# Where the normed values lie, and latents before context in the joint projections

## The chip, the cores and the metric

The kernel runs on one core of a Trainium2 chip. The metric is the time of one execution in device microseconds (us); three runs of the kernel before took 2563.52 to 2567.49 us, median 2566.14. Lower is better. TensorE multiplies matrices (a product streams up to 512 columns of a "moving" operand past 128x128 loaded values); VectorE, ScalarE and GpSimd work elementwise; SyncE issues the transfers.

## The reference

Two blocks in a row on 512 latent tokens beside 256 context tokens, model width 1024, float32. The first block has a feed-forward network, a mixer of retention and gated linear attention, and a second network (latents alone); the second has a matrix-memory mixer of four heads and one attention layer. Each stage begins with a norm, scaled and shifted by a condition, and its result is what all projections of the stage read:

```python
def rms_norm(x, w):
    y = xf * lax.rsqrt(jnp.mean(xf * xf, axis=-1, keepdims=True) + EPS)
    return (y * w.astype(jnp.float32)).astype(x.dtype)
def modulate(h, shift, scale):
    return h * (1.0 + scale[:, None, :]) + shift[:, None, :]
def swiglu(h, w1, w3, w2):
    return (jax.nn.silu(h @ w1) * (h @ w3)) @ w2
...
x = x + 0.5 * m_l[2] * swiglu(modulate(rms_norm(x, norm1_w[i]), m_l[0], m_l[1]), ffn1_w1[i], ffn1_w3[i], ffn1_w2[i])
ctx = ctx + 0.5 * m_c[2] * swiglu(modulate(rms_norm(ctx, norm1_w[i]), m_c[0], m_c[1]), ...)
y_l, y_c = token_mixing(modulate(rms_norm(x, norm2_w[i]), ...), modulate(rms_norm(ctx, norm2_w[i]), ...), w_in[i], ...)
```

## The kernel before, in words

Values lie by feature: 8 tiles k of 128 features, and 768 columns, of which 0 to 255 are context (CTX) and 256 to 767 latents (LAT). Every large product is made of three, for accuracy: an operand is split into a high part that TensorE takes as fp32r, and a low part (the rest). The normed values are hh and hl, weights wh and wl, and the product is wh·hh + wh·hl + wl·hh. In a network's second projection u (uh, ul) takes the place of h; in the matrix-memory block m_yh and m_yl, in retention r_yh and r_yl.

Weights come in chunks of 256 columns (m). SyncE loads chunk m into one of two stage buffers, ScalarE writes wh (L385), VectorE wl (L393), and each waits until the buffer's chunk before, m-2, is used. `by_features` (L411) multiplies a chunk: for each half f (128 of its columns), for each k, for each of the three terms, first the context's 256 columns into half of bank b[2] (L444), then the latents' 512 columns into bank b[f] (L447). Two sets of three banks, SETS, take turns. After a half, the semaphore gemm for (m, f) is raised, and after both also that of m; whoever reads the context waits for that of m. Between the halves `mid` is called, and after each k `beside`, which let small products of other work in. With `ready` (the first chunk on new values) the latents of both halves come first (L422), then the context (L434), each k waiting for its values.

Where only latents are wanted, L447 stands alone: in the second network, for retention's queries, keys and gates, and in attention (L3617). Products with tokens as loaded operand (L1556, L4089) move the weights. The joint form, context and latents in turn, has 2112 pairs on hh and hl: 20 chunks of the first network, one of the gated attention's keys (GK), 7 chunks of keys and queries and 16 of output gates in the matrix-memory block, 48 pairs a chunk. It has 324 pairs on u and 288 on m_y.

In the matrix-memory block `ml_pe` (L3298) multiplies for each head h the keys' chunk (MK), the gate rows (L2903, `gate_rows_pe`), and the queries' chunk (MQ). For h of 1 to 3 MQ has as `mid` `normed_output_pe` (L3128): two products of ones and a diagonal matrix, which spread the scale of the previous head's output. They wait for m_out_diag, which VectorE raises at L3126, after the reciprocal L3124, after ScalarE's root (L553). ScalarE comes to that root, in program order, after the wh of a chunk that waits for MK's end, the copies of keys, the gate rows and the exponentials of the gate's weights.

In memory each partition's buffers follow one another from byte 1152. By that arithmetic stage, wh, wl, direct, hh and hl begin on multiples of 128 bytes, and rows and token tiles in them too. The shared area, in which u, r_y and m_yh lie (and at times two weight buffers, third), begins 32 bytes behind such a multiple. The attention's output a_yh lies where hh does.

Of the kernel before, what the change touches and what calls it, by code (L numbers as in the profile page):

```python
# [3 lines left out]
T = 768  # L4
C = 256
L = 512
# [221 lines left out]
        self.n, self.counted = 0, True  # L228


class Tally:


# [7 lines left out]
def build(nc, wts, vec, con, conds, xin, cin, cin2, out):  # L241
# [5 lines left out]
    F32, F32R = mybir.dt.float32, mybir.dt.float32r  # L247
# [13 lines left out]
    base = 1152  # L261

    def at(name, shape, dt, off):
        return nc.alloc_sbuf_tensor_at(name, shape, dt, offset=base + off)

    x = at("x", [128, 8, T], F32, 0)
    o = 24576
# [3 lines left out]
    o += 16384  # L271
    wl = [at(f"wl{i}", [128, 2048], F32R, o + 8192 * i) for i in range(2)]
    o += 16384
    DIRECT = o
    direct = [at(f"direct{i}", [128, 1024], F32, o + 4096 * i) for i in range(3)]
    o += 12288
    HREG = o
    hh = at("hh", [128, 8, T], F32R, o)
    hl = at("hl", [128, 8, T], F32R, o + 24576)
    o += 49152  # L280
    con0 = at("con0", [128, 512], F32, o)
    o += 2048
    vecs = at("vecs", [128, NVEC], F32, o)
# [12 lines left out]
    MVA = o  # L296
    o += 4096
    cb = at("cb", [128, 8, 6], F32, o)
    o += 192
    AREA = o  # L300
    ASIZE = 228192 - o

    def area(name, shape, dt, off):
        n = 4
# [10 lines left out]
    bank = [stack.enter_context(nc.psum_tensor(f"ps{i}", [128, 512], F32)) for i in range(8)]  # L315
    CTX, LAT = slice(0, C), slice(C, T)
# [33 lines left out]
    group = [area(f"group{i}", [128, 8, 256 * len(g)], F32, 16384 * i) for i, g in enumerate(GROUPS)]  # L350
    group_in = [[signal(f"group_in{i}_{j}", 16) for j in range(4 if i == 0 else 2)] for i in range(len(GROUPS))]

    rows_at = [DIRECT, DIRECT + 4096, DIRECT + 8192, AREA + 40960, AREA + 45056, HREG + 18432]
    rows_chunk = [at(f"first{i}", [128, 1024], F32, o_) for i, o_ in enumerate(rows_at)]
    rows_chunk_in = [signal(f"first_in{i}", 16) for i in range(len(rows_at))]

# [5 lines left out]
    gemm = signal("gemm")  # L362
# [41 lines left out]
    def empty(pe, *banks):  # L404
        for b in banks:
            if emptied[b]:
                s, key = emptied[b]
                pe.wait_ge(*s.at(*key))
                emptied[b] = None

    def by_features(pe, m, b, sh, sl, lat, ctx, ready=None, mid=None, beside=None):  # L411

        nk, h, l = parts(m)
        pe.wait_ge(*w_low.at(m))
        empty(pe, *([b[0], b[1]] if lat else []), *([b[2]] if ctx else []))
        if ready:

            for k in range(nk):
                ready(0, k)
                for f in range(2):  # L420
                    for a, (w, s) in enumerate(((h, sh), (l, sh), (h, sl))):
                        i = pe.matmul(bank[b[f]][:, :], w[:, k, 128 * f:128 * f + 128], s[:, k, LAT], start=k == 0 and a == 0,  # L422
                                      stop=k == nk - 1 and a == 2, skip_group_check=True)
            i.then_inc(*gemm.up(m, 0))
            gemm.also(m, 1)
            gemm.also(m)
            if mid:
                mid()
            if ctx:
                for f in range(2):  # L430
                    for k in range(nk):
                        ready(1, k)
                        for a, (w, s) in enumerate(((h, sh), (l, sh), (h, sl))):
                            i = pe.matmul(bank[b[2]][:, 256 * f:256 * f + 256], w[:, k, 128 * f:128 * f + 128], s[:, k, CTX],  # L434
                                          start=k == 0 and a == 0, stop=k == nk - 1 and a == 2, skip_group_check=True)
                i.then_inc(*gemm.up(m))
            return
        for f in range(2):
            cols = slice(128 * f, 128 * f + 128)
            for k in range(nk):  # L440
                for a, (w, s) in enumerate(((h, sh), (h, sl), (l, sh))):
                    st, en = k == 0 and a == 0, k == nk - 1 and a == 2
                    if ctx:
                        i = pe.matmul(bank[b[2]][:, 256 * f:256 * f + 256], w[:, k, cols], s[:, k, CTX], start=st, stop=en,  # L444
                                      skip_group_check=True)
                    if lat:
                        i = pe.matmul(bank[b[f]][:, :], w[:, k, cols], s[:, k, LAT], start=st, stop=en, skip_group_check=True)  # L447
                if beside and k < nk - 1:
                    beside((nk - 1) * f + k)
            i.then_inc(*gemm.up(m, f))  # L450
            if f == 0 and mid:
                mid()
        gemm.also(m)

    def by_tokens(pe, m, b, sh, sl, tiles, mid=None):

# [39 lines left out]
    class Norm:  # L496


        def __init__(self, n, lo, off, slot, parts=None):
            self.n, self.lo, self.slot, self.parts = n, lo, slot, parts  # L500
            self.acc = area(f"n_acc{n}", [128, T], F32, off)
            self.sq = [area(f"n_sq{i}_{n}", [128, T], F32, off + 3072 * (i + 1)) for i in range(2)]
            self.dg = area(f"n_dg{n}", [128, T], F32, off + 9216)
            NORMS[n] = self
# [152 lines left out]
    sq1 = [area(f"n_sq1_{i}", [128, T], F32, 55296 + 3072 * i) for i in range(4)]  # L657
    factor1 = area("factor1", [128, T], F32, 67584)

    row1 = [at(f"row1_{i}", [128, 512], F32, HREG + 43008 + 2048 * i) for i in range(2)]  # L660
    M1first = M1[:, 0:16, :].rearrange("p (a k) s -> p a k s", a=2)
    bias_first = bias1[:, 0:32].rearrange("p (a k s) -> p a k s", a=2, k=8)
    row_copied = signal("row_copied")
# [789 lines left out]
    o = (o + 64 + 31) // 32 * 32  # L1453
# [481 lines left out]
    class Lat:  # L1935
# [5 lines left out]
        def __getitem__(self, i):  # L1941
            p, k, s = i
            return self.t[p, k, s.start - C:s.stop - C]
# [1549 lines left out]
    o = 25088  # L3493
# [857 lines left out]
```

## Time and profile before

| | |
|---|---|
| three runs, median | 2566.14 us |
| the profiled execution, and its span | 2565.66 us, 2563.9 us |
| TensorE busy | 2523.1 us, 98% |
| VectorE, ScalarE, GpSimd busy | 1301.4, 824.4, 229.3 us |
| chain that ended last | TensorE 92%, VectorE 5%, ScalarE 2% |
| mean granted clock of TensorE | 0.996 |

The span is the profiled stretch, 1.8 us less than the execution's own time. A product's length in the trace reaches over the next one's start, since products are pipelined: the pace is read from the starts. Starts of single rows are given to 0.01 us, so a pace is read best from two rows far apart with a known number of products between them. A row of the timeline with a count joins several instructions of one kind.

### The profile page before, as it was taken

What the parts mean: (1) busy time and instruction counts of PE and PEld (TensorE: products, weight loads), DVE (VectorE), ACT (ScalarE), POOL (GpSimd) and SP (SyncE); (2) the same over time, 40 slices, a digit from 0 to 9 for tenths busy, and PEclk for the clock granted to TensorE, in tenths of its full rate; (3) what the DMA queues carried; (4) which work ended last, traced back from release to release, by engine and by line L of the source; (5) the groups of instructions that cost most, each with busy time, mean ns of one, the idle gap of its engine ahead of it and who ended that gap; (6) DMA issues with size and microseconds to landing.
All of it is one profiled execution on the core that took longest, in us unless ns stands there. A gap on an engine that the chain in (4) does not pass through costs nothing.

```text
span 2563.9 us, 31059 instructions
## 1 busy us (share of the span) xinstructions
PE 2523.1 (98%) x13030; PEld 2019.1 (79%) x13030; DVE 1301.4 (51%) x2065; ACT 824.4 (32%) x1172; POOL 229.3 (9%) x186
## 2 busy tenths in 40 slices
PE   7999999999999999999999999999999999999999
PEld 3888888888757878888888687887787788687766
DVE  6665433426346766767747433422432332476663
ACT  3211112124243354232324323122222312245663
POOL 0100001002111002000000110110210101210001
PEclk9999999999999999999999999999999999999999
DMA  7334343312111112545432110210111021011001
GB/s 294 115 134 157 128 152 119 128 50 82 59 42 65 52 50 81 183 174 191 162 115 91 50 42 17 74 66 17 50 66 50 17 83 66 17 67 66 34 34 50
DMA packets 45114, 223.55 MB, mean 87 GB/s; under 512 B 4736, under 2 KB 6960, under 8 KB 30128
## 3 DMA queue, kind: packets, MB, share of 16 engines
q1 hardware_dynamic: 43008, 215.24, 23.5%
q10 hardware_dynamic: 1968, 6.34, 0.7%
q8 instruction: 103, 1.69, 0.3%
q14 instruction: 35, 0.29, 0.0%
HBM read 219.46 MB, written 2.10 MB: 86 GB/s over the span
## 4 chain that ended last, share of the span: by engine, by line
PE 92%; DVE 5%; ACT 2%; issue 1%; POOL 0%; DMA 0%; SPq 0%; DVEq 0%; ACTq 0%; POOLq 0%
PE ps L447 41%; PE ps L444 13%; PE ps L1556 8%; PE ps L422 3%; PE ps L3617 3%; PE ps L3164 3%; PE ps L2953 2%; PE ps L1257 2%; PE ps L876 1%; PE ps L3734 1%; PE ps L3833 1%; PE ps L3857 1%; DVE wl L393 1%; PE ps L2543 1%; PE ps L2079 1%
## 5 line engine op out<-in xcount | busy, mean ns | idle before, releaser
L393 DVE TENSOR_TENSOR wl<-stage,wh 128x2048 fp32r<-128x2048 f32 (+2 forms) x155 | 325.8, 2102 | 478.7 <-ACT wh L385 478.5
L447 PE MATMUL ps<-hh,wh 128*128 128x512 f32 x1120 | 442.0, 395 | 0.0
L447 PE MATMUL ps<-hl,wh 128*128 128x512 f32 x1120 | 441.4, 394 | 0.0
L447 PE MATMUL ps<-hh,wl 128*128 128x512 f32 x1120 | 441.1, 394 | 0.0
L385 ACT ACTIVATE wh<-stage 128x2048 fp32r<-128x2048 f32 (+2 forms) x155 | 267.2, 1724 | 456.3 <-PE ps L447 338.5
L447 PEld LDWEIGHTS ps<-hh,wl 128*128 128x128 f32 x1120 | 210.5, 188 | 48.5
L447 PEld LDWEIGHTS ps<-hh,wh 128*128 128x128 f32 x1120 | 210.6, 188 | 47.2 <-issue 1.2
L447 PEld LDWEIGHTS ps<-hl,wh 128*128 128x128 f32 x1120 | 210.4, 188 | 47.4 <-issue 1.2
L650 DVE CUSTOM_DVE_ANT_0 left<-direct,cond_rows,vecs 128x1024 bf16<-128x1024 f32 x168 | 207.0, 1280 | 0.0
L444 PE MATMUL ps<-hh,wh 128*128 128x256 f32 x688 | 197.6, 287 | 1.2 <-DVE m_X L2977 1.2
L444 PE MATMUL ps<-hh,wl 128*128 128x256 f32 x688 | 194.1, 282 | 0.0
L444 PE MATMUL ps<-hl,wh 128*128 128x256 f32 x688 | 192.9, 280 | 0.0
L444 PEld LDWEIGHTS ps<-hh,wh 128*128 128x128 f32 x688 | 130.6, 190 | 5.7 <-issue 5.5
L444 PEld LDWEIGHTS ps<-hh,wl 128*128 128x128 f32 x688 | 130.0, 189 | 0.0
L444 PEld LDWEIGHTS ps<-hl,wh 128*128 128x128 f32 x688 | 130.0, 189 | 0.0
L1556 PE MATMUL ps<-wh,hh 128*128 128x512 f32 x288 | 119.1, 413 | 0.0
L1209 POOL TENSOR_TENSOR ul<-sl,uh 128x768 fp32r<-128x768 f32 (+1 forms) x28 | 43.6, 1575 | 819.9 <-ACT uh L1097 819.8
L1556 PE MATMUL ps<-wh,hl 128*128 128x512 f32 x288 | 113.4, 394 | 0.0
L1556 PE MATMUL ps<-wl,hh 128*128 128x512 f32 x288 | 113.3, 394 | 0.0
L447 PE MATMUL ps<-uh,wh 128*128 128x512 f32 x240 | 94.6, 394 | 0.0
L1097 ACT ACTIVATE uh<-sl 128x512 fp32r<-128x512 f32 (+1 forms) x42 | 30.7, 734 | 198.2 <-DVE sl L1160 138.2
L447 PE MATMUL ps<-ul,wh 128*128 128x512 f32 x240 | 94.3, 393 | 0.0
(608 smaller groups left out, 4723.7 us busy)
## 6 DMA issues: line engine op xcount, KB each, us to landing
stage<-wts SPq DMA_DIRECT2D x110, 1024.0 KB, 4.8
direct<-wts SPq DMA_DIRECT2D x104, 512.0 KB, 4.2
stage<-wts SPq DMA_DIRECT2D x24, 768.0 KB, 4.3
stage<-wts SPq DMA_DIRECT2D x22, 512.0 KB, 3.3
group<-wts SPq DMA_DIRECT2D x6, 512.0 KB, 6.3
first<-wts SPq DMA_DIRECT2D x6, 512.0 KB, 9.7
x<-xin SPq DMA_DIRECT2D x4, 512.0 KB, 7.7
group<-wts SPq DMA_DIRECT2D x2, 1024.0 KB, 9.7
```

The source lines that it names most:

```text
L385: act.activation(split(m)[0][:, 0:w], stage[m % 2][:, 0:w], ACT.Copy).then_inc(*w_high.up(m))
L393: dve.tensor_tensor(l[:, 0:w], stage[m % 2][:, 0:w], h[:, 0:w].bitcast(F32), SUB).then_inc(*w_low.up(m))
L422: i = pe.matmul(bank[b[f]][:, :], w[:, k, 128 * f:128 * f + 128], s[:, k, LAT], start=k == 0 and a == 0, stop=k == nk - 1 and a == 2, skip ...
L444: i = pe.matmul(bank[b[2]][:, 256 * f:256 * f + 256], w[:, k, cols], s[:, k, CTX], start=st, stop=en, skip_group_check=True)
L447: i = pe.matmul(bank[b[f]][:, :], w[:, k, cols], s[:, k, LAT], start=st, stop=en, skip_group_check=True)
L650: dve.tensor_tensor_reduce(left[n % 2][:, :], chunk[:, :], rows_of[:, s, :], 1.0, bias[:, s:s + 1], MUL, ADD, to[:, s:s + 1]).then_inc(*mo ...
L1209: pool.tensor_tensor(z.ul[:, k, z.lo:T], z.sl[(2 * p + f) % 4][:, z.lo:T], z.uh[:, k, z.lo:T].bitcast(F32), SUB).then_inc(*u_low_pool.up(n ...
L1257: j = pe.matmul(bank[tail_bank(i, ft)][:, 0:p.n], w[:, k, cols], s[:, k, p.cols], start=k == 0 and a == ends[0], stop=k == 3 and a == ends ...
L1556: i = pe.matmul(bank[t][:, :], s[:, 4 * j + k, 128 * t:128 * t + 128], u[:, k, :], start=j == 0 and k == 0 and a == 0, stop=j == 1 and k = ...
L2953: i = pe.matmul(bank[bb][:, 0:hi_ - lo], mk[:, f, 128 * J:128 * J + 128], mq[:, f, lo:hi_], start=f == 0, stop=f == 1, skip_group_check=True)
L3164: pe.matmul(bank[b[0]][:, :], mv_[:, J, fs], wpart(J, C, T), start=J == 0, stop=J == 5, skip_group_check=True)
L3617: i = pe.matmul(bank[f][:, :], u[:, k, 128 * f:128 * f + 128], s[:, k, LAT], start=k == 0 and a == 0, stop=k == 7 and a == 2, skip_group_c ...
```

## The change

1. `hh` and `hl` become pairs of tiles, wrapped in a class `Sides` that picks by column: latents hhl and hll, [128, 8, 512], on multiples of 128 bytes, and context hhc and hlc, [128, 8, 256], 64 bytes behind one. 
2. `direct` moves by 64 bytes. The shared area is put on a multiple of 64; worked out as above it begins 64 bytes behind a multiple of 128, where it was 32 behind. The buffers of the first rows (rows_at, row1) move so that they still lie over tiles of h that are written late.
3. In the joint form of `by_features` the latents of both halves come first, then the context of both. `mid` and `beside` stay beside the latents. The semaphore of m is raised after the context, as its readers need.

```diff
+class Sides:
+
+    def __init__(self, tiles):
+        self.context, self.latents = tiles
+
+    def __getitem__(self, i):
+        p, k, s = i
+        if s.stop <= C:
+            return self.context[p, k, s]
+        return self.latents[p, k, slice(s.start - C, s.stop - C)]
+
+
...
-    DIRECT = o
-    direct = [at(f"direct{i}", [128, 1024], F32, o + 4096 * i) for i in range(3)]
-    o += 12288
+    DIRECT = o + 64
+    direct = [at(f"direct{i}", [128, 1024], F32, DIRECT + 4096 * i) for i in range(3)]
+    o += 12416
     HREG = o
-    hh = at("hh", [128, 8, T], F32R, o)
-    hl = at("hl", [128, 8, T], F32R, o + 24576)
-    o += 49152
+    hh = Sides([at("hhc", [128, 8, C], F32R, o + 32832), at("hhl", [128, 8, L], F32R, o)])
+    hl = Sides([at("hlc", [128, 8, C], F32R, o + 41024), at("hll", [128, 8, L], F32R, o + 16384)])
+    o += 49280
...
     cb = at("cb", [128, 8, 6], F32, o)
-    o += 192
+    o += 192 + (-(base + o + 192)) % 64
     AREA = o
-    ASIZE = 228192 - o
+    ASIZE = 228224 - o
...
-    rows_at = [DIRECT, DIRECT + 4096, DIRECT + 8192, AREA + 40960, AREA + 45056, HREG + 18432]
+    rows_at = [DIRECT, DIRECT + 4096, DIRECT + 8192, AREA + 40960, AREA + 45056, HREG + 12288]
...
-        empty(pe, *([b[0], b[1]] if lat else []), *([b[2]] if ctx else []))
+        empty(pe, b[0], b[1], *([b[2]] if ctx else []))
...
             cols = slice(128 * f, 128 * f + 128)
             for k in range(nk):
                 for a, (w, s) in enumerate(((h, sh), (h, sl), (l, sh))):
-                    st, en = k == 0 and a == 0, k == nk - 1 and a == 2
-                    if ctx:
-                        i = pe.matmul(bank[b[2]][:, 256 * f:256 * f + 256], w[:, k, cols], s[:, k, CTX], start=st, stop=en,
-                                      skip_group_check=True)
-                    if lat:
-                        i = pe.matmul(bank[b[f]][:, :], w[:, k, cols], s[:, k, LAT], start=st, stop=en, skip_group_check=True)
+                    i = pe.matmul(bank[b[f]][:, :], w[:, k, cols], s[:, k, LAT], start=k == 0 and a == 0, stop=k == nk - 1 and a == 2,
+                                  skip_group_check=True)
                 if beside and k < nk - 1:
                     beside((nk - 1) * f + k)
             i.then_inc(*gemm.up(m, f))
             if f == 0 and mid:
                 mid()
         gemm.also(m)
+        if ctx:
+            for f in range(2):
+                cols = slice(128 * f, 128 * f + 128)
+                for k in range(nk):
+                    for a, (w, s) in enumerate(((h, sh), (h, sl), (l, sh))):
+                        i = pe.matmul(bank[b[2]][:, 256 * f:256 * f + 256], w[:, k, cols], s[:, k, CTX], start=k == 0 and a == 0,
+                                      stop=k == nk - 1 and a == 2, skip_group_check=True)
+            i.then_inc(*gemm.up(m))
...
-    row1 = [at(f"row1_{i}", [128, 512], F32, HREG + 43008 + 2048 * i) for i in range(2)]
+    row1 = [at(f"row1_{i}", [128, 512], F32, HREG + 28672 + 2048 * i) for i in range(2)]
```

Engines other than TensorE have the same instructions in the same order. On TensorE the number of products is the same too. In the order of TensorE's instructions, at the second pair of chunks of the first network, one k of the joint form reads before (hh_59 and hl_60 are the moving operand, wh0_52 and wl0_54 the loaded one, ps2 the bank of the context, ps0 that of a half's latents; the digits behind are the program's numbering):

```order
L444 MATMUL ps2<-hh_59,wh0_52 128x256
L447 MATMUL ps0<-hh_59,wh0_52 128x512
L444 MATMUL ps2<-hl_60,wh0_52 128x256
L447 MATMUL ps0<-hl_60,wh0_52 128x512
L444 MATMUL ps2<-hh_59,wl0_54 128x256
L447 MATMUL ps0<-hh_59,wl0_54 128x512
```

and now, where the same chunk's latents end and its context begins (ps1 is the bank of the second half's latents):

```order
L454 MATMUL ps1<-hhl_60,wh0_52 128x512
L454 MATMUL ps1<-hll_62,wh0_52 128x512
L454 MATMUL ps1<-hhl_60,wl0_54 128x512
L467 MATMUL ps2<-hhc_59,wh0_52 128x256
L467 MATMUL ps2<-hlc_61,wh0_52 128x256
L467 MATMUL ps2<-hhc_59,wl0_54 128x256
```

The 24 context products of each half have moved from between the latents to behind both halves.

In head 1 of the matrix-memory block, around the call between the halves of the queries' chunk (m_EM holds the diagonal, con the ones), it reads before:

```order
L447 MATMUL ps3<-hl_60,wh1_53 128x512
L444 MATMUL ps5<-hh_59,wl1_55 128x256
L447 MATMUL ps3<-hh_59,wl1_55 128x512
L3131 MATMUL ps6<-m_EM_192,con0_61 128x512
L3132 MATMUL ps7<-m_EM_192,con0_61 128x256
L444 MATMUL ps5<-hh_59,wh1_53 128x256
L447 MATMUL ps4<-hh_59,wh1_53 128x512
```

and now:

```order
L454 MATMUL ps3<-hhl_60,wh1_53 128x512
L454 MATMUL ps3<-hll_62,wh1_53 128x512
L454 MATMUL ps3<-hhl_60,wl1_55 128x512
L3147 MATMUL ps6<-m_EM_194,con0_63 128x512
L3148 MATMUL ps7<-m_EM_194,con0_63 128x256
L454 MATMUL ps4<-hhl_60,wh1_53 128x512
L454 MATMUL ps4<-hll_62,wh1_53 128x512
```

Ahead of that call stood 48 products of the chunk, and now stand 24, the latents alone.

## Rows read from the trace of the kernel before

**Rows 1.** The page: TensorE busy; the chain that ended last, by engine, line
```profile
PE 2523.1 (98%) x13030; PEld 2019.1 (79%) x13030; DVE 1301.4 (51%) x2065; ACT 824.4 (32%) x1172; POOL 229.3 (9%) x186
...
PE 92%; DVE 5%; ACT 2%; issue 1%; POOL 0%; DMA 0%; SPq 0%; DVEq 0%; ACTq 0%; POOLq 0%
PE ps L447 41%; PE ps L444 13%; PE ps L1556 8%; PE ps L422 3%; PE ps L3617 3%; PE ps L3164 3%; PE ps L2953 2%; PE ps L1257 2%; PE ps L876 1%; PE ps L3734 1%; PE ps L3833 1%; PE ps L3857 1%; DVE wl L393 1%; PE ps L2543 1%; PE ps L2079 1%
```

**Rows 2.** By line and form, TensorE: count, busy us, mean ns, idle
```profile
L447 PE MATMUL ps<-hh,wh 128*128 128x512 f32 x1120 | 442.0, 395 | 0.0
...
L447 PE MATMUL ps<-uh,wh 128*128 128x512 f32 x240 | 94.6, 394 | 0.0
```

**Rows 3.** TensorE's timeline, first FFN, pairs in turn: start us, length us
```profile
199.12 0.28 PE L444 MATMUL ps<-hh,wh 128*128 128x256 f32 x1
...
300.88 0.40 PE L422 MATMUL ps<-uh,wh 128*128 128x512 f32 x1
```

**Rows 4.** TensorE's timeline, an output gate of the matrix-memory block, in turn
```profile
1686.48 0.28 PE L444 MATMUL ps<-hl,wh 128*128 128x256 f32 x1
...
1693.77 0.28 PE L444 MATMUL ps<-hl,wh 128*128 128x256 f32 x1
```

**Rows 5.** TensorE's timeline, second FFN, latents alone: of u, then of h
```profile
1062.13 0.40 PE L422 MATMUL ps<-uh,wh 128*128 128x512 f32 x1
...
1095.73 0.40 PE L447 MATMUL ps<-hh,wh 128*128 128x512 f32 x1
...
1150.17 0.39 PE L2628 MATMUL ps<-con,c_acc 128*128 128x1 f32 x3
```

**Rows 6.** TensorE's timeline, first FFN: context of u alone, then pairs
```profile
309.29 0.28 PE L434 MATMUL ps<-uh,wh 128*128 128x256 f32 x1
...
313.53 0.28 PE L444 MATMUL ps<-uh,wh 128*128 128x256 f32 x1
...
350.97 0.28 PE L444 MATMUL ps<-hh,wh 128*128 128x256 f32 x1
```

**Rows 7.** TensorE's timeline, attention values: 256 columns of weights moving
```profile
2275.81 0.28 PE L4089 MATMUL ps<-wh,hh 128*128 128x256 f32 x1
...
2278.69 0.59 PE L3563 MATMUL ps<-a_ksq,con 128*128 128x512 f32 x1
```

**Rows 8.** TensorE's timeline, head 1: gate rows, first half of queries, spread
```profile
1582.43 1.55 PE L2903 MATMUL ps<-m_RR,c_sel 8*128 8x512 f32 x4
1583.91 0.39 PE L444 MATMUL ps<-hh,wh 128*128 128x256 f32 x1
...
1592.35 0.61 PE L3131 MATMUL ps<-m_EM,con 128*128 128x512 f32 x1
```

**Rows 9.** Timelines of ScalarE and of VectorE in the same time
```profile
1582.54 1.06 ACT L385 ACTIVATE wh<-stage 128x1024 fp32r<-128x1024 f32 x1 [11.17 <-PE ps L447]
...
1589.43 1.28 ACT L553 ACT_TABLE_LOAD   x1
1590.73 0.21 ACT L553 ACTIVATE cb<-cb 128x6 f32<-128x6 f32 x1
...
1590.97 0.19 DVE L3124 RECIPROCAL cb<-cb 128x6 f32<-128x6 f32 x1 [3.45 <-ACT cb L553]
1591.19 0.96 DVE L558 TENSOR_TENSOR m_EM<-con,cb 128x768 f32<-128x768 f32 x1
```

**Rows 10.** TensorE's timeline near the start: a pause, products after it
```profile
27.53 0.41 PE L835 MATMUL ps<-con,row 2*128 2x2 f32 x4 [0.68 <-ACT row L711]
30.81 0.47 PE L876 MATMUL ps<-hh,wh 128*128 128x512 f32 x1 [2.88 <-DVE hl L789]
...
35.48 0.63 PE L876 MATMUL ps<-hl,wh 128*128 128x512 f32 x1
35.91 0.63 PE L876 MATMUL ps<-hh,wh 128*128 128x512 f32 x1
```

**Rows 11.** Window of that stretch: busy us by engine, granted clock (0.50), DMA
```profile
31.90:38.60 6.70, 5.09 (x16) 3.79 (x15) 5.82 (x7) 4.39 (x5) 0.00 (x0) 0.50 1.02 409
```

## The prediction

> **What bounds the kernel now.** I read the page's busy times first, then the chain of waits. TensorE is busy for 98% of the span and carries 92% of the chain, over half of it at the two lines of the joint form and of latents alone, L447 and L444 [rows 1]. So the time is the number of products times their pace, and a change that keeps the number can only act through the pace, or through a pause. The lengths in the groups by line (395 and 394 ns [rows 2]) are no pace, since products overlap. I read the paces off the timeline, from the starts of rows far apart and the count between them, all at the full clock of 2.4 GHz (the span's mean granted clock is 0.996):
>
> - context and latents in turn, hh and hl: 288 pairs in 101.76 us, 353.3 ns a pair [rows 3]; in other chunks 21 pairs in 7.29 us, 347.1 ns [rows 4];
> - latents of u alone, 32 bytes behind a multiple of 128: 144 in 33.60 us, 233.3 ns; of hh and hl alone, on the multiple: 240 in 54.44 us, 226.8 ns [rows 5];
> - 256 columns alone: 36 of u in 4.24 us, 117.8 ns [rows 6]; 24 on a multiple of 128, 2.88 us, 120.0 ns [rows 7];
> - u in turn: 108 pairs in 37.44 us, 346.7 ns [rows 6].
>
> At 2.4 GHz 512 and 256 columns are 213.3 and 106.7 ns. The rest, 13 to 20 ns for latents, is what depends on place and order. These are the two things that the change touches.
>
> **Part 1, latents first.** The 2112 pairs of the joint form on hh and hl become 2112 latent products alone, at their old place, whose pace the trace has (226.8 ns), and 2112 context products alone, 64 bytes behind a multiple, whose pace no row has. Call it c. Bounds: below, 106.7 ns, the columns at the full clock. Above, the aligned 120.0, and if 64 is worse than any place seen, as much more as u's latents pay for theirs (6.5 ns), 126.5. The nearest rows are the 117.8 at 32 bytes and the 120.0 at none; the one farther from the multiple is faster, and I take 116.5, a little on from it. Reading each chunk of the timeline, 1296 pairs run at the pace of [rows 3] and 816 at that of [rows 4] (output gates of heads 1 to 3, the second chunk of those heads, GK, and the chunk whose weights lie in the area). So 1296 x (353.3 - 226.8 - 116.5) = 1296 x 10.0 = 13.0 us, and 816 x 3.8 = 3.1 us. The 324 pairs of u gain 346.7 - 343.3 = 3.4 ns if their latents come to 226.8 (next part), 1.1 us; the 288 of m_y are taken like them, 1.0 us.
>
> **Part 2, the area 64 behind instead of 32.** 924 latent products read the area alone (L422 240, L447 396 of u and 96 of r_y, the two tails 192). They run at 233.3 ns where aligned ones run at 226.8 [rows 5]. Bounds at 64: no gain (233.3) or the aligned pace, with one step more the other way, 239.8, as the far end. 2048 bytes from an offset of 32 touch one 64-byte stretch more than from 0, and from 64 they don't; one such stretch is 16 columns, 6.7 ns, which is just the difference. I take 226.8: 924 x 6.5 = 6.0 us. The 492 products of 256 columns there (108 + 96 + 192 + 96) go from 117.8 to 116.5, 0.6 us.
>
> The Trainium skill speaks against both parts. "SBUF — State Buffer", Door 1, gives SBUF 16-byte cachelines: 32 and 64 are both multiples of 16, so by that rule the offset is worth nothing, the sum loses its 6.0 and 0.6, and context keeps the dearer pace: rival 4 works that out from rows. "TensorE: Matmul & The Clock Gate", Step-by-step, gives TensorE two independent read ports, so that loading the next weights takes nothing from the moving operand. The trace does not agree: 233.3 against 226.8 are the same products but for the offset [rows 5].
>
> **Part 3, what is late next.** ScalarE, VectorE, GpSimd and SyncE keep their instructions and order. Their reads of a half's latents may start earlier, and those of context wait for the chunk's end, as they already did. Weight buffers are freed at the chunk's end, as before. But one wait of TensorE moves forward. In heads 1 to 3 the spread (L3131) stands between the halves of the queries' chunk, and with the change only 24 latents stand ahead of it in the chunk, not 24 pairs. Before, in head 1, keys' end let ScalarE begin its weights at 1582.54; it came to its root at 1590.73, and VectorE's diagonal ended at 1591.19 + 0.96 = 1592.15 [rows 9]. The spread started at 1592.35 [rows 8], so the diagonal came 0.2 us before it. None of that chain gets shorter: its start is the keys' chunk's end, and ScalarE works through it with no gap over 0.1 us. TensorE will come earlier: gate rows until 1583.91 [rows 8], then 24 x 0.2268 + 0.11 for the first = 5.55 us, so at 1589.46. It waits until about 1592.2, 2.7 us, and behind it in TensorE's order stand the second half, the context and all that follows. The other two heads show the same rows within 0.1 us. Three times 2.74 is 8.2 us lost. Between nothing (if the diagonal came early) and 8.8 I take 8.2.
>
> A pause has a second price, the clock. Near the start TensorE paused from 27.53 + 0.41 to 30.81, and then ran at half clock, with 0.43 us between 512-column starts [rows 10, 11]. I count nothing for it: these pauses are shorter and lie among dense products. If each of the three did bring a stretch as long as half of that one, 3.4 us at 0.43 instead of 0.227 would lose 1.6 us, 4.8 in all. The Trainium skill, "TensorE: Matmul & The Clock Gate", HAM oscillation, warns of pauses between dense bursts; if it bit here the sum would be those 4.8 us higher, and of this length no pause among dense products is in the trace.
>
> Other places where small products come beside or between: GK's log gates, the column sums in the keys' chunks and head 0's denominators. By the same timelines their inputs and banks stand ready well before the new times too, so I count nothing; should one be late, it would cost what it waits, once. What these edits add elsewhere (direct 64 bytes on, rows_at, row1) lies on transfers and on VectorE under a TensorE that is 98% busy. Should VectorE's operations or the first transfers get slower there, only the first 30 us would show it.
>
> **Sum.** 13.0 + 3.1 + 1.1 + 1.0 + 6.0 + 0.6 = 24.8 us gained, 8.2 lost: 16.6. From the profiled execution's own 2565.66 us this gives 2549.1, so 2549. That execution lies 0.5 us under the median of the runs, which changes nothing.
>
> **Rivals.**
> 1. Context at 64 goes half the way from 120.0 to the floor, c = 113.3. Then 3216 products of 256 columns (2112 + 324 + 288 + 492) gain 3.2 ns more, 10.3 us: 2539. For it: 32 bytes already save 2.2 ns. Against: no product alone in the trace does it.
> 2. 64 is like a multiple of 128: c = 120.0, latents 226.8. Then 3216 x 3.5 = 11.3 us of the gain are gone: 2560. For it: in 64-byte stretches both places are the same.
> 3. The pause does not come, since ScalarE's chain is shortened by copies that could start earlier: 8.2 us better, 2541. Against: those copies stand behind the wait for the chunk's end in ScalarE's order.
> 4. Slower: places off the multiple of 128 keep the dear pace, in the area as on context (c = 120.0, area's latents 233.3), and the pauses stand. Of the 24.8 remain 24.8 - 11.3 - 6.0 - 612 x 6.5 ns (4.0) = 3.5 us, under the 8.2 of pauses: 2570, and up to 2575 with the clock. It decides the sign from the point where the paces give less than 8.2 us. Against: it needs 128 bytes to be the unit, and [rows 6, 7] show 256 columns faster off the multiple.
> **How the numbers follow.** The forecast 0.46, rival 1 0.20, rival 2 0.14, rival 3 0.08, rival 4 0.12. A measurement here can tell about 0.2%, 5 us, from no change. The forecast with 3 ns of c either way is 2539 to 2559. The range for 8 in 10 takes in rivals 1 to 3 but leaves out most of 4 and the far side of 1: 2536 to 2563. Faster by over 0.2% (under 2561): forecast, 1, 3 and most of 2, 0.80. Within: the rest of 2, a little of 4 and of the forecast, 0.11. Slower 0.09.
>
> **What would show it.** In the profile after, latents of the joint form should start 226.8 ns apart; the context block shows c directly, its length over 48 a chunk. The u products at L422 should read 227 rather than 233. In heads 1 to 3 the spread should be preceded by a pause of 2.7 us, put down to VectorE's diagonal, and ScalarE's chain from keys' end to root should still take 8.4 us. The granted clock around those pauses shows whether the price is double. A context pace over 121 ns or a latent pace in the area of 233 would prove the forecast wrong; so would pauses at other waits.

## The result, and the profile after

| | before | after |
|---|---|---|
| median (5 runs each, side by side) | 2566.38 us | 2578.87 us |
| range of the runs | 2563.52 to 2567.75 | 2576.46 to 2580.39 |
| ratio, with its 95% interval | | 1.0053, 1.0041 to 1.0064 |
| profiled execution, span, granted clock | 2565.66, 2563.9 us, 0.996 | 2576.46, 2574.7 us, 0.994 |

The changed kernel is 0.5% slower. The prediction said 2549, 2536 to 2563: wrong in sign and outside its range. In the kernel before the weights wh begin at byte 42112 and h at 87168; both are 128 behind a multiple of 256. In the changed kernel h's latents begin at 87296, a multiple of 256. That turned out to be the point.

The page after, answering [rows 1]: TensorE's busy time and the chain, by engine and line. L454 is now the latents, L467 the context.

```profile
PE 2527.5 (98%) x13030; PEld 2013.0 (78%) x13030; DVE 1302.1 (51%) x2065; ACT 826.0 (32%) x1172; POOL 230.3 (9%) x186
...
PE 90%; DVE 5%; ACT 3%; issue 1%; POOL 0%; DMA 0%; SPq 0%; DVEq 0%; ACTq 0%; POOLq 0%
PE ps L454 40%; PE ps L467 12%; PE ps L1572 8%; PE ps L434 3%; PE ps L3633 3%; PE ps L3180 3%; PE ps L2969 2%; PE ps L1273 2%; PE ps L892 1%; PE ps L3750 1%; PE ps L3849 1%; DVE wl L405 1%; PE ps L3873 1%; PE ps L2559 1%; PE ps L2095 1%
```

That page is no verdict: it looks like the one before, as it must when only the pace changed. TensorE's timeline after, in the first network (start us, length us), the same stretch as [rows 3] and [rows 6]:

```profile
198.97 0.39 PE L454 MATMUL ps<-hhl,wh 128*128 128x512 f32 x1
...
210.13 0.28 PE L467 MATMUL ps<-hhc,wh 128*128 128x256 f32 x1
...
298.78 0.40 PE L434 MATMUL ps<-uh,wh 128*128 128x512 f32 x1
...
307.03 0.28 PE L446 MATMUL ps<-uh,wh 128*128 128x256 f32 x1
...
311.27 0.40 PE L454 MATMUL ps<-uh,wh 128*128 128x512 f32 x1
...
348.75 0.39 PE L454 MATMUL ps<-hhl,wh 128*128 128x512 f32 x1
```

48 latents of h take 11.16 us, 232.5 ns each, where 226.8 was forecast. Six chunks of 48 + 48 take 99.81 us, 346.6 ns for a latent and a context product (before 353.3, forecast 343.3), so context is at 114.1, cheaper than the 116.5 taken. The 108 products of each size on u take 37.48 us, and took 37.44 in turn: nothing gained there. The second network, answering [rows 5]:

```profile
1060.54 0.40 PE L434 MATMUL ps<-uh,wh 128*128 128x512 f32 x1
...
1093.51 0.40 PE L454 MATMUL ps<-hhl,wh 128*128 128x512 f32 x1
...
1149.28 0.50 PE L2644 MATMUL ps<-con,c_acc 128*128 128x1 f32 x4
```

144 latents of u: 229.0 ns (before 233.3, forecast 226.8). 240 latents of h: 55.77 us, 232.4 ns, where the same instructions, in the same order, took 226.8 before. What differs is where they lie: their first byte, and 2048 bytes from one k to the next where it was 3072. Head 1, answering [rows 8]: TensorE's last product ahead of the spread, the spread, and the group of waits over all heads (us in total, times, longest).

```profile
1587.72 0.40 PE L454 MATMUL ps<-hhl,wl 128*128 128x512 f32 x1
1590.66 1.10 PE L3147 MATMUL ps<-m_EM,con 128*128 128x512 f32 x2 [2.54 <-DVE m_EM L574]
```

```profile
PE ps L3147 <- DVE m_EM L574: 7.6, 3, 2.5
```

ScalarE and VectorE of that place, answering [rows 9]:

```profile
1580.90 1.06 ACT L397 ACTIVATE wh<-stage 128x1024 fp32r<-128x1024 f32 x1 [10.99 <-PE ps L467]
...
1587.80 1.28 ACT L569 ACT_TABLE_LOAD   x1
1589.09 0.21 ACT L569 ACTIVATE cb<-cb 128x6 f32<-128x6 f32 x1
```

```profile
1589.55 0.96 DVE L574 TENSOR_TENSOR m_EM<-con,cb 128x768 f32<-128x768 f32 x1
```

From the keys' end to the root is 8.2 us, as before. The pause is 2.94 us from start to start, and a product's own 0.23 is in it: 2.7, as forecast, three times. Behind the pauses of heads 2 and 3 the granted clock was 0.50, half of 2.4 GHz (window; its length in us, TensorE busy, granted clock; then two starts in the first window):

```profile
1808.44:1811.86 3.42, 3.42 (x10) 0.50 0.00 0
2026.90:2030.31 3.41, 3.41 (x10) 0.50 0.00 0
```

```profile
1809.60 0.63 PE L454 MATMUL ps<-hhl,wl 128*128 128x512 f32 x1
1810.03 0.63 PE L454 MATMUL ps<-hhl,wh 128*128 128x512 f32 x1
```

0.43 us a product is the pace at half clock of [rows 10]. Behind head 1's pause the clock stayed full.

### The profile page after: what moved, and what is told of

It reads as the page before. It is cut to its first block, busy times and chain, and to the rows that moved or that the text cites. A ratio compares the mean times of both kernels' runs of the same rounds, so it can differ in the third digit from the quotient of the medians.

```text
span 2574.7 us, 31059 instructions
## 1 busy us (share of the span) xinstructions
PE 2527.5 (98%) x13030; PEld 2013.0 (78%) x13030; DVE 1302.1 (51%) x2065; ACT 826.0 (32%) x1172; POOL 230.3 (9%) x186
## 4 chain that ended last, share of the span: by engine, by line
PE 90%; DVE 5%; ACT 3%; issue 1%; POOL 0%; DMA 0%; SPq 0%; DVEq 0%; ACTq 0%; POOLq 0%
PE ps L454 40%; PE ps L467 12%; PE ps L1572 8%; PE ps L434 3%; PE ps L3633 3%; PE ps L3180 3%; PE ps L2969 2%; PE ps L1273 2%; PE ps L892 1%; PE ps L3750 1%; PE ps L3849 1%; DVE wl L405 1%; PE ps L3873 1%; PE ps L2559 1%; PE ps L2095 1%
## 5 line engine op out<-in xcount | busy, mean ns | idle before, releaser
L454 PE MATMUL ps<-hhl,wh 128*128 128x512 f32 x1120 | 452.4, 404 | 1.2 <-DVE m_X L2993 1.2
L454 PE MATMUL ps<-hll,wh 128*128 128x512 f32 x1120 | 444.2, 397 | 0.0
L454 PE MATMUL ps<-hhl,wl 128*128 128x512 f32 x1120 | 444.1, 397 | 0.0
L454 PEld LDWEIGHTS ps<-hhl,wh 128*128 128x128 f32 x1120 | 212.3, 190 | 53.8 <-issue 6.8
L454 PEld LDWEIGHTS ps<-hhl,wl 128*128 128x128 f32 x1120 | 212.0, 189 | 50.7
L454 PEld LDWEIGHTS ps<-hll,wh 128*128 128x128 f32 x1120 | 212.5, 190 | 48.3 <-issue 1.2
L467 PE MATMUL ps<-hhc,wl 128*128 128x256 f32 x688 | 190.2, 276 | 0.0
L467 PE MATMUL ps<-hhc,wh 128*128 128x256 f32 x688 | 190.2, 276 | 0.0
L467 PE MATMUL ps<-hlc,wh 128*128 128x256 f32 x688 | 190.2, 276 | 0.0
L467 PEld LDWEIGHTS ps<-hhc,wh 128*128 128x128 f32 x688 | 129.3, 188 | 2.0
L467 PEld LDWEIGHTS ps<-hlc,wh 128*128 128x128 f32 x688 | 129.1, 188 | 1.9
L467 PEld LDWEIGHTS ps<-hhc,wl 128*128 128x128 f32 x688 | 129.2, 188 | 0.0
L454 PE MATMUL ps<-uh,wh 128*128 128x512 f32 x240 | 94.9, 395 | 0.0
L454 PE MATMUL ps<-uh,wl 128*128 128x512 f32 x240 | 94.0, 392 | 0.0
L454 PE MATMUL ps<-ul,wh 128*128 128x512 f32 x240 | 93.3, 389 | 0.0
```

## The experiments

Times are medians, ratios stand against runs of the kernel before beside them. "Distance" is the moving operand's first byte minus the loaded one's, modulo 256.

### Products alone, by place

```python
for k in range(8):
    for a, (u, p) in enumerate(((wh, 0), (wh, 1), (wl, 0))):      # 0: high part of the moving operand, 1: low part
        mm(bank[f], u[:, k, cols], s[p][:, k, :])                  # u and s begin at chosen bytes
...
go(mm, 128, 128, 2, "wide")   # L304: moving 128, loaded 128; L305: 160, 128; L306: 192, 128; L312: 128, 0; L317: 64, 64
```

> This kernel leaves out the whole computation and writes zeros: TensorE does products of zeros alone, in stretches of 96 (a few of 48 or 288) whose loaded and moving operands begin at chosen bytes modulo 1024; every stretch has a line of its own, and high and low parts take turns as in the kernel. Theory A (pace is set by the address of the moving operand modulo 256, together with that of the loaded one): moving 128 with loaded 128 gives about 227 ns a product of 512 columns, moving 0 with loaded 128 about 232.7, 160 about 233, 192 about 229; 256 columns at 64 give 114 and at 128 120. If it is the relation between the two that counts, moving 0 with loaded 0 gives 227 again; if the moving address alone, 232.7. Theory B (the address doesn't count, the pace of the changed kernel's latents comes from the tile's shape or from other engines' traffic): all stretches of one form show the same pace within 1 ns.

TensorE's timeline: first product of some stretches; 96 products stand between one row and the next.

```profile
181.32 0.40 PE L304 MATMUL ps<-hh,wh 128*128 128x512 f32 x1
...
203.09 0.40 PE L305 MATMUL ps<-hh,wh 128*128 128x512 f32 x1
...
225.49 0.40 PE L306 MATMUL ps<-hh,wh 128*128 128x512 f32 x1
...
247.48 0.40 PE L307 MATMUL ps<-hh,wh 128*128 128x512 f32 x1
...
358.46 0.40 PE L312 MATMUL ps<-hh,wh 128*128 128x512 f32 x1
...
380.86 0.40 PE L313 MATMUL ps<-hh,wh 128*128 128x512 f32 x1
```

Line 304 (both at 128) takes 21.77 us, 226.8 ns; line 305 (160) 233.3; 306 (192) 229.1; 312 (moving 128 again, but loaded 0) 233.3. Lines 304 and 312 move the same bytes, and only the loaded operand lies elsewhere. The same reading of all stretches, in ns a product (good to 0.1):

| distance | 0 | 32 | 64 | 96 | 128 | 160 | 192 | 224 |
|---|---|---|---|---|---|---|---|---|
| 512 columns, loaded at 128 | 226.7 | 233.4 | 229.0 | 233.5 | 233.3 | 234.2 | 233.3 | 233.2 |
| 512 columns, loaded at 0 | 226.8 | 233.4 | 229.0 | 233.5 | 233.4 | 234.2 | 233.2 | 233.2 |
| 512 columns, loaded at 64 | 226.9 | | 229.1 | | 232.5 | | 233.4 | |
| 256 columns, loaded at 128 | 119.9 | 117.8 | 117.8 | 119.9 | 118.7 | 118.7 | 113.4 | 118.3 |

Moving at 384 gave 226.8 as at 128, and 256 and 512 gave 233.3 as 0 did. With 3072 bytes from k to k, as h had before, distances 0 and 128 gave 227.2 and 233.2. So theory A holds, in its form with the relation: the pace follows the distance modulo 256, to within 1 ns (distance 128 reads 232.4 to 233.4, in these stretches and in the kernels). It explains the readings of both kernels: h before at distance 0 (226.8), after at 128 (233.3 here, 232.4 there); the area's latents before at distance 32 (233.3), after at 64 (229.0); context of h after at 192 (113.4). "A multiple of 128" was never the unit.

### The changed kernel, shifted by 128 bytes

```diff
-    o += 12416
+    o += 12544
```

> The changed kernel with all that lies behind direct moved on by 128 more bytes, so that latents begin 128 behind a multiple of 256 again, as in the kernel before. Theory A (address modulo 256): the latents of h alone go from 232.7 back to 226.8 ns; some 3984 such products by 5.9 ns and 864 products with tokens loaded by 3.8 ns are 27 us, so about 2552 us, if the area (now 64 behind a multiple of 256) keeps 229 ns; with 233 there, 2556. Theory B (shape of the tiles, 2048 bytes from k to k where it was 3072, or a neighbour): 232.7 ns stays and the time is that of the changed kernel, 2579. The pauses of 2.9 us in heads 1 to 3 stand in both.

2570.72 us, ratio 1.0024 (1.0015 to 1.0032). The place in the second network again:

```profile
1065.89 0.39 PE L454 MATMUL ps<-uh,wh 128*128 128x512 f32 x1
...
1091.09 0.39 PE L454 MATMUL ps<-hhl,wh 128*128 128x512 f32 x1
...
1145.51 0.50 PE L2644 MATMUL ps<-con,c_acc 128*128 128x1 f32 x4
```

240 latents of h in 54.42 us: 226.8 ns, the pace of before, by 128 bytes alone. Theory B falls. The time missed the expected 2552 since the shift moved the rest too: u's latents went to distance 192 and to 233.3 ns (108 in 25.20 us), context of h to distance 64 and from 113.9 to 117.9. Those two cost 4 and 8 us of the 22 won. Of the 7 us that are still missing the clock explains about 4: stretches at half clock cost some 16 us in this profiled execution and some 12 in the changed kernel's (an estimate from the starts of all products in and outside them).

### Latents first, all places as before

The diff is that of `by_features` in the change, with nothing else.

> The kernel before with latents first in the joint form and nothing else, all places as before. Theory A: latents of h alone at 226.8 ns, context alone on a multiple of 128 at about 120 ns, u's latents stay at 233.3. Against the pairs that is 1296 x 6.5 + 816 x 0.3 = 8.7 us gained, u and m_y lose 612 x 4.4 ns = 2.7 us, and three pauses of 2.9 us take 8.7: about 2569. Theory C (latents first is itself what makes latents 232.7 ns, in the joint form): 2112 x 5.9 ns = 12.5 us more, about 2581.

2573.54 us, 1.0032 (1.0019 to 1.0045). Latents of h stand at 227 ns, context at 119.8, u's latents at 233.3: theory A, and C falls. The time is 4 us above the expected 2569; its runs had a mean granted clock of 0.991 to 0.996, and the one at 0.996 took 2567.4. The order alone gains nothing here: over the whole trace the pace is worth some 5 us, less than the 8 of the pauses, and half clock costs this profiled execution some 7 us more than the kernel before.

### The spread later

```diff
-                            (lambda: normed_output_pe(pe, h - 1)) if h and j else None,
-                            (lambda n: sums_beside(pe, h - 1, n)) if h and j == 0 else None)
+                            None, ((lambda n: n == 11 and normed_output_pe(pe, h - 1)) if j else (lambda n: sums_beside(pe, h - 1, n))) if h else None)
```

> The changed kernel with the two spread products of heads 1 to 3 moved from between the halves of the queries' chunk to behind the fifth k of the second half, 3.4 us later on TensorE. Theory A (the pause is a plain wait for VectorE's diagonal, and nothing else is late behind it): the three gaps of 2.93 us vanish, 8.6 us less, and the stretches of 3.4 us at half clock behind two of them as well, 1.6 us each: 2567. If the clock falls all the same: 2570. Theory D (what follows the spread, the normed output for the projection, comes late in its turn): another wait of 2 to 3 us a head takes its place, 2576 to 2580.

2566.10 us, 1.0005 (0.9996 to 1.0014), so 12.8 us less than the changed kernel. TensorE at the spread of head 1, and the first rows of all its waits (L3147 is in none):

```profile
1591.41 0.39 PE L454 MATMUL ps<-hhl,wl 128*128 128x512 f32 x1
1591.64 1.02 PE L3147 MATMUL ps<-m_EM,con 128*128 128x512 f32 x2
```

```profile
PE ps L859 <- DVE n_sq L768: 11.5, 3, 10.5
PE ps L892 <- DVE hll L805: 2.9, 1, 2.9
PE ps L454 <- DVE m_X L2993: 2.4, 2, 1.2
PE ps L2095 <- DVE g_Wd L2105: 1.8, 7, 0.3
```

The pause is gone and nothing took its place: theory A. The profiled executions of the two kernels lie 10.6 us apart. TensorE is idle 7.5 us less, the pace is the same within 0.1 us, and the rest, 3 us, is the clock: the two stretches of 3.4 us at half clock behind the spread are gone. Outside them, and the last 2 us aside, both have the same 20.5 us at half clock, and so has the kernel before.

So the pauses bring the half clock, which the traces of the other kernels bear out. In the kernel shifted by 128 bytes all three pauses are followed by it, and where the spread waits for nothing, as in the kernel with places by distance and the later spread (below), it doesn't come. Windows behind the three pauses of the shifted kernel, then one around the spread of head 2 in the other:

```profile
1584.99:1588.40 3.41, 3.41 (x6) 0.50 0.00 0
1803.45:1806.86 3.41, 3.36 (x6) 0.50 0.00 0
2021.90:2025.31 3.41, 3.19 (x6) 0.50 0.00 0
```

```profile
1780.00:1815.00 35.00, 35.00 (x196) 1.00 0.05 16
```

In the ten profiled executions of whole kernels, three spreads in each, 9 of the 12 spreads that wait (2.5 to 2.65 us of idle time each) have such a stretch beginning within 1.3 us of their own start, and none of the 18 that don't wait has one. Why three pauses brought none is open.

### High and low parts at places of their own

```python
go(mm, (128, 128), (128, 128), 1, "wide")   # L300: loaded high, low; moving high, low
go(mm, (128, 128), (128, 192), 1, "wide")   # L301, and so on through 64 combinations, then 256 columns
```

> This kernel leaves out the whole computation and writes zeros, as the stretches of products before did: 64 stretches of 48 products with 512 columns, and 64 with 256, where the loaded high part stays 128 behind a multiple of 256 and the loaded low part, the moving high part and the moving low part each take 0, 64, 128 and 192. Theory A2 (a product pays for the distance from the operand loaded beside it to the moving one, modulo 256): with the parts alike the paces of the earlier stretches return (226.8, 229.0, 233.3 and 233.2 ns for distances 0, 64, 128, 192; 119.9, 117.8, 118.6, 113.4 for 256 columns), and mixed ones lie between them, none under 226 or 113. Rival: it is the operand loaded during a product (the next product's) that counts, so that a low part at another place than the high one can make all three kinds cheap at once: some mixed stretch under 225 ns.

First products of two stretches of 48 and of the one behind:

```profile
91.14 0.39 PE L300 MATMUL ps<-hh,wh 128*128 128x512 f32 x1
...
102.02 0.39 PE L301 MATMUL ps<-hh,wh 128*128 128x512 f32 x1
...
1012.33 0.28 PE L401 MATMUL ps<-hh,wh 128*128 128x256 f32 x1
...
1017.77 0.28 PE L402 MATMUL ps<-hh,wh 128*128 128x256 f32 x1
```

All alike gives 226.7 ns (L300), the best of 64; the next best has 228.9, the worst 235.6. With 256 columns the best is 113.3 (L401), the worst 122.3. The rival's stretch under 225 isn't there. Not as expected: mixed ones go beyond the range of the unmixed.

### Places by distance, and both remedies

```diff
-    DIRECT = o + 64
+    DIRECT = o
-    o += 12416
+    o += 12288
-    hh = Sides([at("hhc", [128, 8, C], F32R, o + 32832), at("hhl", [128, 8, L], F32R, o)])
-    hl = Sides([at("hlc", [128, 8, C], F32R, o + 41024), at("hll", [128, 8, L], F32R, o + 16384)])
-    o += 49280
+    hh = Sides([at("hhc", [128, 8, C], F32R, o + 32960), at("hhl", [128, 8, L], F32R, o)])
+    hl = Sides([at("hlc", [128, 8, C], F32R, o + 41152), at("hll", [128, 8, L], F32R, o + 16384)])
+    o += 49344
-    o += 192 + (-(base + o + 192)) % 64
+    o += 192 + (128 - (base + o + 192)) % 256
```

> The changed kernel with places chosen by the distance to the weights modulo 256: latents of h, the tiles in direct and the area at distance 0 (128 behind a multiple of 256, as the weights lie), context of h at distance 192 (64 behind such a multiple). The spread stays between the halves. Theory A2: latents of h 226.8 ns where they were 232.7 (3984 products, 23.5 us), tokens as loaded operand 3 ns less (864, 2.6 us), the area's latents 226.8 for 229.0 (924, 2.0 us) and its 256 columns 119.9 for 117.8 (492, 1.0 us dearer), context of h stays 113.8, the pauses in heads 1 to 3 grow by 0.15 us each: about 2552. Theory B2 (only the absolute place counts, so that area and context behave as in the shifted kernel): context 118 ns, and 2560.

2563.69 us, 1.0000 (0.9991 to 1.0010): 15 us less than the changed kernel, 12 more than expected.

```profile
196.95 0.40 PE L454 MATMUL ps<-hhl,wh 128*128 128x512 f32 x1
...
207.86 0.28 PE L467 MATMUL ps<-hhc,wh 128*128 128x256 f32 x1
...
213.51 0.39 PE L454 MATMUL ps<-hhl,wh 128*128 128x512 f32 x1
```

Latents are at 227.2 ns, u's at 226.7, as expected. But 48 context products take 5.65 us, 117.8 ns, and the changed kernel's took 113.4 to 114.1, at the very same bytes (120128 and 128320) with the same loaded operand: 8 of the 12 us. B2 expected 118, but for a reason (absolute place) that the same bytes rule out. The law of distances alone was not the whole.

With the later spread as well:

> The places by distance as in the kernel beside it, and the spread of heads 1 to 3 behind the fifth k of the second half. Theory A2 with the pause as a plain wait: the gain of the places (27 us) and that of the later spread (12.8 us measured) add: 2579 - 27 - 13 = 2539. Rival (the faster latents make the diagonal late again even at the fifth k, since TensorE arrives 0.25 us earlier there, or other inputs come late): pauses of some 2 us a head, 2545.

2549.90 us, 0.9944 (0.9931 to 0.9957), against 2539 expected: the gains add (13.8 us for the spread), and the same 8 us are missing. The spread waits for nothing.

### What decides between 113 and 118

```python
wide(mm); narrow(mm, m=64)          # L316, L317: latents at distance 0, then 256 columns at 64
wide(mm); narrow(mm, m=240)         # L338, L339
wide(mm, m=0); narrow(mm)           # L341, L342: latents at distance 128, then 256 columns at 64
```

> This kernel leaves out the whole computation and writes zeros. Open is why context of h, at the same addresses as in the changed kernel (64 behind, loaded operand at 128), ran at 113.8 ns there and at 117.8 in the kernel with places by distance, where the latents ahead of it run at distance 0. Here 48 products of 512 columns at distance 0 precede 48 of 256 columns in each stretch. Theory E (the pace is a rhythm that products fall into, and the products ahead decide which one): 256 columns at 64 give 117.8 behind latents at distance 0 and 113.4 behind latents at distance 128 or others, and a single product of another size or another order of the three terms at the start can bring the 113.4 back. Rival F (something in the full kernel, another engine's traffic or a tile's place, makes the 117.8): 113.4 in all of them.

```profile
169.19 0.28 PE L317 MATMUL ps<-hh,wh 128*128 128x256 f32 x1
...
174.85 0.39 PE L318 MATMUL ps<-hh,wh 128*128 128x512 f32 x1
...
351.76 0.28 PE L339 MATMUL ps<-hh,wh 128*128 128x256 f32 x1
...
357.24 0.39 PE L340 MATMUL ps<-hh,wh 128*128 128x512 f32 x1
...
379.34 0.28 PE L342 MATMUL ps<-hh,wh 128*128 128x256 f32 x1
...
384.78 0.39 PE L343 MATMUL ps<-hh,wh 128*128 128x512 f32 x1
```

The same 48 products at 64 take 5.66 us behind latents at distance 0 (L317, 117.8 ns) and 5.44 behind latents at distance 128 (L342, 113.4). Theory E, with no other engine at work; F falls. Latents at distances 160, 192 and 32 also lead to 113.4 to 113.6, those at 64 to 117.7. One further product of 64 or 192 columns in between brings the 113 back, one of 2, 16 or 128 doesn't, and neither does another order of terms, halves or k. Of sixteen places, 240 was the best behind latents at distance 0 (L339: 114.2).

Beside it stood the kernel before with the area alone at distance 0:

```diff
-    o += 192
+    o += 192 + (128 - (base + o + 192)) % 256
```

> The kernel before with the shared area alone moved, to 128 behind a multiple of 256, the distance 0 to the weights; order, spread and all else as before. Theory A2: 924 latent products of the area alone go from 233.3 to 226.8 ns, 6.0 us; its 612 pairs in turn (346.7 and 352 ns) come to the 353.3 or 347.1 that pairs on h show, between 4 us lost and 1.5 gained; its 192 products of 256 columns alone lose 0.4: 2560 to 2564. Rival (the rhythm that they enter makes them dear in spite of distance 0): no change, 2565 to 2566.

2565.77 us, 1.0002 (0.9992 to 1.0012). u's latents alone went to 226.7 ns, but its pairs in turn from 346.7 to 353.4, 2.2 us of the 6 lost again; the rest hides in runs whose clock lay between 0.993 and 0.997 (2559.5 at 0.997, 2569.4 at 0.994). As a time it is inconclusive. The three runs of the kernel before at 0.997, beside it, took 2560.9 to 2562.1, the two of this one 2559.5 and 2559.8: at equal clock some 2 us less.

### Context at 240

The diff is against the kernel with places by distance (the later spread is in both):

```diff
-    hh = Sides([at("hhc", [128, 8, C], F32R, o + 32960), at("hhl", [128, 8, L], F32R, o)])
-    hl = Sides([at("hlc", [128, 8, C], F32R, o + 41152), at("hll", [128, 8, L], F32R, o + 16384)])
+    hc = at("hc", [128, 16 * C + 8], F32R, o + 32864)
+    hhc, hlc = (hc[:, 4 + 8 * C * i:4 + 8 * C * i + 8 * C].rearrange("p (k s) -> p k s", k=8) for i in range(2))
+    hh = Sides([hhc, at("hhl", [128, 8, L], F32R, o)])
+    hl = Sides([hlc, at("hll", [128, 8, L], F32R, o + 16384)])
```

> The kernel with places by distance and the later spread, with context of h moved from 64 to 240 modulo 256 (distance 112 to the loaded operand). In the stretches of products alone, behind latents at distance 0, context at 64 ran at 117.8 ns and at 240 at 114.2. Theory E (the rhythm that the products ahead lead into decides, and 240 leads into the cheap one): 2112 context products at 114.2 instead of 117.5 ns are 7 us less than the kernel beside it, 2543 where that has 2550. Rival (VectorE and ScalarE write context on addresses that are multiples of 16 bytes alone and get slower, or the full kernel's rhythm differs): context at 117 to 119 ns or the same time within 3 us.

> The kernel with places by distance and the later spread once more, beside the one with context at 240, for a comparison on one chip: 2550 again, context of h at 117.5 ns.

```profile
196.73 0.40 PE L456 MATMUL ps<-hhl,wh 128*128 128x512 f32 x1
...
207.63 0.39 PE L469 MATMUL ps<-hc,wh 128*128 128x256 f32 x2
...
213.11 0.39 PE L456 MATMUL ps<-hhl,wh 128*128 128x512 f32 x1
```

Context runs at 114.2 ns, latents stay at 227.2. 2547.37 us, 0.9927 (0.9911 to 0.9943), against 2553.49, 0.9950 (0.9933 to 0.9966), of the kernel beside it: 6 us, the expected 7 less a little. The two intervals overlap, so the times alone don't settle it; the pace does, and so do runs at equal clock. It is the fastest kernel here, 18 us under the one before. Its six runs are 2538.9 at a clock of 0.998, 2542.1 (0.996), 2545.8 (0.995), 2548.9 and 2549.0 (0.993), 2553.7 (0.991): a thousandth of mean clock is worth 2.1 us. At 0.996 the kernel beside it took 2547.7 and 2548.1.

## Why the prediction was wrong, step by step

**The step that failed** is in part 1: the latents stay "at their old place, whose pace the trace has (226.8 ns)". I looked at the place modulo 128, and the diff keeps that; but it moves h from 87168 to 87296, from distance 0 to distance 128. All latents of h became dearer: 2112 in the joint form by 5.7 ns (12.0 us of the gain gone), the 1296 alone by 5.6 ns (7.3 us lost, forecast nothing), and with them attention's products, the first chunks and those with tokens loaded (some 6 us, forecast nothing). Shown by products alone, by the shift of 128 bytes, and by the kernels with places by distance.

**Context at 64 (part 1).** Taken 116.5, measured 114.1 in [rows 3]'s stretch, near rival 1: 2112 x 2.4 = 5.1 us better. That the gain of the joint form was 1296 x 6.7 + 816 x 0.5, some 9 us instead of 16, is these two together. The 113 was partly luck: it holds behind latents at the wrong distance, and not behind the cheap ones.

**The area (part 2).** Forecast 6.5 ns on 924 products, measured 4.3 (distance 64): 4.0 us instead of 6.0. My count of 64-byte stretches matched the 6.5 ns of [rows 5] by chance and had the wrong cause: it has no loaded operand in it. u's pairs, forecast to gain 1.1 us, gained nothing: 347.0 ns (37.48 us for 108) where they had 346.7 in turn. Nor did u's 256 columns alone, 117.8 ns before and after, where 116.5 was forecast. m_y's pairs gained 1.4 us for 1.0. The Trainium skill, "SBUF — State Buffer", Door 1, gives SBUF 16-byte cachelines. No run here follows them as a rule for these products: distances of 32, 64 and 128 bytes are all whole cachelines, and cost 6.7, 2.3 and 6.6 ns over the 226.7 of distance 0.

**The pause (part 3).** Right in place, cause and size: three of 2.7 us, put down to VectorE's diagonal. Its second price, the clock, was put at nothing, because "these pauses are shorter and lie among dense products". That term failed too: two of three pauses brought 3.4 us at half clock, 1.6 us each by the prediction's own estimate, 3.2 in all. The clock is no accident beside them, as the half clock outside these stretches is 20.5 us in both profiled executions.

**The ledger** of the profiled executions, 10.8 us apart: joint form 8 to 9 gained, area 4 to 5 gained, latents alone 7 lost, idle time 7 lost (the pauses' 7.6, less a little elsewhere), clock 3 lost; that is 4 to 5 lost. The rest is h at its new distance elsewhere. Read from the starts at full clock over the whole trace, the products with tokens loaded lost 3.3 us (864 at 235.0 ns before, 238.8 after), attention's queries and gates 1.5, its output 0.9, the first chunks 0.5. These 6 us close the sum.

**The rivals.** Rival 4 was the nearest in time (2570) and right that the sum of paces would fall short of the pauses, but its reason, 128 bytes as the unit of the moving operand, was not the one. Missing was a rival with the loaded operand in it, although [rows 5 to 7] could not tell an absolute place from a relation.

## What to carry to other kernels

Where TensorE is the bound and its products follow each other closely, each with a load of its own as here, place the moving operand by its distance to the loaded one: the same remainder modulo 256 for 512 fp32r columns; for 256 columns measure, since what runs ahead decides too. A pace read in one kernel holds only for the addresses of both operands, so print them before and after an edit, modulo more than the edit speaks of. When fewer or faster products stand ahead of one that waits for another engine, move it back by as much: a short pause costs itself and, here in 9 of 12 cases, a stretch at half clock.

## What the runs showed of the hardware

- The pace of fp32r products depends on the distance of the two operands modulo 256: 226.7 to 234.2 ns for 512 columns, 113.4 to 119.9 for 256 ([rows 5 to 7] give four points of it). The best of either length is the columns at full clock plus 13.4 or 6.7 ns.
- At half clock neither the distance nor the 13.4 ns is seen: 512 columns start 426 to 427 ns apart, which is the columns at 1.2 GHz alone, at distance 0 (kernel before), at 128 (changed kernel) and at 192 (m_y in the shifted one).
- The pace is a rhythm with memory: the same products at the same bytes settle at 113.4 or 117.8 ns for as long as 48 products, by what ran ahead. Steady rhythms repeat exactly (227, 226, 227). Why is open.
- Pauses of 2.7 us in dense work were followed by 3.4 us at half clock in 9 of 12 cases.
- Runs of one kernel differ by up to 0.007 in mean clock, 15 us, which is more than most edits here; the clock belongs beside every time. Over the runs of all nine kernels a thousandth goes with about 2.3 us (a fitted estimate). Compared by that fit at equal clock, the changed kernel is 8 us above the one before, the order alone 2 above, the shifted kernel 1 below, the area alone 2 below, places by distance 7 below, with the later spread 17 to 18, and with context at 240 as well 22. What the pauses cost in clock is left out of these.
